# Keys and three gated attention groups turned by VectorE in 32x32 blocks instead of by TensorE

## What is computed

```
q, k, v, gate = split(h @ w_in)                    # 2048, 256, 256, 2048 columns
q, k = rms_norm(q, q_gain), rms_norm(k, k_gain)    # 32 query heads, 4 key heads of 64
s = q . k * 64**-0.5 + bias[dist]                  # window of 128 positions, blocks of 128
m = max(max(s), sink);  p = exp(s - m)
o = (p / (sum(p) + exp(sink - m))) . v
out = x + (o * silu(gate)) @ w_out
```

## Time and profile before

| | |
|---|---|
| median of 3 runs | 1460.72 us |
| profiled execution | 1460.59 us, of it span 1458.9 us |
| TensorE busy, clock | 99% of the span, granted clock 1.0 of full |
| VectorE busy | 66% |
| ScalarE busy | 48% |
| GpSimd busy | 9% |

### The profile page before, as it was taken

The page is one execution under the profiler, slowest core; times in us unless marked ns, Lnnn a source line. Parts: engine busy times, 40 slices in busy tenths (PEclk is TensorE's granted clock), DMA queues, the critical chain, the costliest instruction groups (busy, mean ns, idle before and its releaser), DMA issues.

```text
span 1458.9 us, 18259 instructions
## 1 busy us (share of the span) xinstructions
PE 1447.7 (99%) x6683; PEld 1195.6 (82%) x6683; DVE 964.6 (66%) x1287; ACT 696.7 (48%) x928; POOL 126.6 (9%) x115
## 2 busy tenths in 40 slices
PE   9999999999999999999999999999999999999999
PEld 7887888888888888888888888887878888888887
DVE  5499978856666554566754556769698566665553
ACT  7444564454444443444443444445555566564432
POOL 2099110000000000000000000000000211200000
PEclk9999999999999999999999999999999999999999
DMA  9755655566665566666655666645555655545562
GB/s 332 221 177 156 196 176 203 199 203 188 201 191 198 187 190 195 192 193 195 191 188 195 189 197 191 194 166 180 195 189 187 220 152 175 156 121 165 172 205 93
DMA packets 141495, 274.04 MB, mean 188 GB/s; under 512 B 8593, under 2 KB 10893, under 8 KB 141304
## 3 DMA queue, kind: packets, MB, share of 16 engines
q1 hardware_dynamic: 139608, 266.49, 58.2%
q0 software_dynamic: 1792, 6.71, 1.5%
q10 hardware_dynamic: 32, 0.01, 0.0%
HBM read 271.02 MB, written 2.15 MB: 187 GB/s over the span
## 4 chain that ended last, share of the span: by engine, by line
PE 89%; DVE 9%; ACT 1%; issue 1%; POOL 0%; ACTq 0%; POOLq 0%
PE acc L1240 28%; PE acc L1242 28%; PE acc L1241 28%; DVE w_lo L781 3%; DVE tile L847 2%; DVE tile L805 1%; PE tp L1491 1%; PE acc L1302 1%; PE tp L1260 1%; PE sp L1472 1%; PE tp L1270 1%; DVE tile L1119 0%; DVE yl L816 0%; ACT w_hi L493 0%; ACT tile L702 0%
## 5 line engine op out<-in xcount | busy, mean ns | idle before, releaser
L781 DVE TENSOR_TENSOR w_lo<-w_raw,w_hi 128x1024 fp32r<-128x1024 f32 x500 | 610.8, 1228 | 423.2 <-ACT w_hi L493 421.1
L493 ACT ACTIVATE w_hi<-w_raw 128x1024 fp32r<-128x1024 f32 x500 | 526.4, 1059 | 581.0 <-PE acc L1242 578.4
L1240 PE MATMUL acc<-w_lo,yh 128*128 128x512 f32 x1184 | 462.7, 391 | 3.6 <-DVE w_lo L781 3.6
L1242 PE MATMUL acc<-w_hi,yl 128*128 128x512 f32 x1184 | 460.8, 389 | 0.0
L1241 PE MATMUL acc<-w_hi,yh 128*128 128x512 f32 x1184 | 460.7, 389 | 0.0
L1240 PE MATMUL acc<-w_lo,hh 128*128 128x512 f32 x784 | 310.4, 396 | 0.6 <-DVE w_lo L781 0.6
L1242 PE MATMUL acc<-w_hi,hl 128*128 128x512 f32 x784 | 305.7, 390 | 0.0
L1241 PE MATMUL acc<-w_hi,hh 128*128 128x512 f32 x784 | 305.2, 389 | 0.0
L1240 PEld LDWEIGHTS acc<-w_lo,yh 128*128 128x128 f32 x1184 | 222.2, 188 | 53.0 <-DVE w_lo L781 6.4
L1242 PEld LDWEIGHTS acc<-w_hi,yl 128*128 128x128 f32 x1184 | 222.2, 188 | 46.6
L1241 PEld LDWEIGHTS acc<-w_hi,yh 128*128 128x128 f32 x1184 | 222.3, 188 | 45.7
(11 more groups left out here) (158 smaller groups left out, 612.2 us busy)
## 6 DMA issues: line engine op xcount, KB each, us to landing
w_raw<-in_w_gate SPq DMA_DIRECT2D x88, 512.0 KB, 3.8
w_raw<-in_w_up SPq DMA_DIRECT2D x88, 512.0 KB, 3.9
w_raw<-in_w_down SPq DMA_DIRECT2D x88, 512.0 KB, 3.8
w_raw<-in_swa_w_in SPq DMA_DIRECT2D x72, 512.0 KB, 3.8
w_raw<-in_w_in SPq DMA_DIRECT2D x64, 512.0 KB, 4.3
w_raw<-in_w_out SPq DMA_DIRECT2D x32, 512.0 KB, 3.8
w_raw<-in_w_ple_gate SPq DMA_DIRECT2D x32, 512.0 KB, 4.3
w_raw<-in_swa_w_out SPq DMA_DIRECT2D x32, 512.0 KB, 4.3
```

The lines of the kernel that those rows point to most:

```text
L493: act.activation(w_hi[:, s % SPL], w_raw[:, s % RAW], ACT.Copy).then_inc(hi_ready, 1)
L781: dve.tensor_tensor(w_lo[:, s % SPL], w_raw[:, s % RAW], w_hi[:, s % SPL].bitcast(F32), ALU.subtract).then_inc(lo_ready, 1)
L1240: pe.matmul(dst, xh[:, f, tk], w_lo[:, s % SPL, k], start=(f == 0), stop=False)
L1242: last = pe.matmul(dst, xl[:, f, tk], w_hi[:, s % SPL, k], start=False, stop=(f == CK * n - 1))
```

## The change

The keys are turned by VectorE: after the chunks (2,2) to (2,5) it turns one quarter each of `tok(2)` into tile 3; TensorE's transposes at (2,3) and ScalarE's copies at (2,6) are gone. TensorE waits for `k_turned` before the first scores. The gated groups 0 to 2 are turned by VectorE too: after the chunks c = 4 to 7 of units 6, 7 and 8 it turns one quarter each of group v-6 into tile 5. ScalarE's high part and VectorE's low part come from that tile at c = 1 of the next unit (before: from PSUM at c = 0). TensorE's transposes at (6,5), (7,5) and (8,5) are gone; TensorE waits for the low parts at chunks 0, 2 and 4 of the first output unit. Group 3 is as before. On VectorE, the turn of a chunk stands in front of `softmax_max(3,2)` at (6,5) and of `weighted(3,0)` at (6,6), and `turned_low` at (7,1) in front of `weighted(3,1)`.

```diff
+T_FFN, T_HID, T_PLE, T_SWA, T_OG = 0, 3, 11, 14, 17
...
@@ ScalarE
-                    if (v, c) == (2, 6):
-                        copy(H_K, tile[3])
...
-                    if c == 0 and v >= 7:
-                        high(H_OG[v - 7], yh[:, 4 * (v - 7):4 * (v - 7) + 4])
+                    if c == 1 and v >= 7:
+                        turned_high(T_OG + v - 7, yh[:, 4 * (v - 7):4 * (v - 7) + 4], turned_in=5)
...
-                    if (j, c) == (0, 0):
-                        high(H_OG[2], yh[:, 8:12])
+                    if (j, c) == (0, 1):
+                        turned_high(T_OG + 2, yh[:, 8:12], turned_in=5)
@@ VectorE
-                        last.then_inc(kd_ready, 1)
-                    if c == 0 and v >= 7:
+                        step(last)
+                    if v == 2 and 2 <= c <= 5:
+                        turn(tok(2), (c - 2,), k_turned if c == 5 else None, turn_in=3)
+                    if c == 1 and v >= 7:
                         q = slice(4 * (v - 7), 4 * (v - 7) + 4)
-                        low(H_OG[v - 7], yl[:, q], yh[:, q])
+                        turned_low(T_OG + v - 7, yl[:, q], yh[:, q], turned_in=5)
...
+                    if c >= 4 and v >= 6:
+                        if c == 4:
+                            dve.wait_ge(og_ready, v - 5)
+                        turn(wide[:, :, CW * (v - 6):CW * (v - 5)], (c - 4,), turned if c == 7 else None, turn_in=5)
                     if c == 5 and 3 <= v <= 6:
                         softmax_max(v - 3, 2)
@@ TensorE
+                if n == 0:
+                    pe.wait_ge(k_turned, 1)
...
-                    if (v, c) == (2, 3):
-                        pe.wait_ge(kd_ready, 1)
-                        to_features(H_K, tok(2))
...
-                    if c == 5 and v >= 6:
-                        pe.wait_ge(og_ready, v - 5)
-                        g = v - 6
-                        to_features(H_OG[g], wide[:, :, CW * g:CW * (g + 1)])
...
-                    if (j, c) == (0, 0):
-                        wait_half_left(pe, H_OG[1] + 1)
-                    if (j, c) == (0, 4):
-                        wait_half_left(pe, H_OG[2] + 1)
+                    if j == 0 and c in (0, 2, 4):
+                        pe.wait_ge(turned_lo, T_OG + c // 2 + 1)
```

More of the change, by code:

```diff
@@ L80 @@
 HALVES += "xx"
-H_K = len(HALVES)
-HALVES += "aa"
-H_Q, H_PT, H_PV, H_OG = {}, {}, {}, {}
+H_Q, H_PT, H_PV = {}, {}, {}
 for _g in range(5):
@@ L95 @@
         H_Q[_g] = len(HALVES); HALVES += "aa"
-    else:
-        H_OG[0] = len(HALVES); HALVES += "xx"
     H_PV[q, 1] = len(HALVES); HALVES += "d"
@@ L100 @@
     H_PV[q, 2] = len(HALVES); HALVES += "d"
-for _g in range(1, 4):
-    H_OG[_g] = len(HALVES); HALVES += "xx"
-T_FFN, T_HID, T_PLE, T_SWA = 0, 3, 11, 14
+H_OG = len(HALVES)
+HALVES += "xx"
+T_FFN, T_HID, T_PLE, T_SWA, T_OG = 0, 3, 11, 14, 17
 ROUNDS = ((0, 0, 8, 1), (1, 0, 4, 2), (1, 4, 4, 2))
@@ L263, in build @@
         kv_ready = sem("kv_ready")
-        kd_ready = sem("kd_ready")
         q_squares = sem("q_squares")
@@ L275, in build @@
         turned_lo = sem("turned_lo")
+        k_turned = sem("k_turned")
         stored = sem("stored")
@@ L513, in high, with turned_high @@
                     last.then_inc(feat_hi, 1)
-            def turned_high(n, dst, gains=None, lap=ONCE):
+            def turned_high(n, dst, gains=None, lap=ONCE, turned_in=TURN):
                 act.wait_ge(turned, n + 1 + lap.turns)
                 if gains is None:
-                    last = act.activation(dst, feat(TURN), ACT.Copy)
+                    last = act.activation(dst, feat(turned_in), ACT.Copy)
                 else:
@@ L764, in _ @@
                     if (j, c) == (0, 5):
-                        high(H_OG[3], yh[:, 12:16])
+                        high(H_OG, yh[:, 12:16])
         @block.vector
@@ L796, in low, with turn @@
                     last.then_inc(tp_left["d"], 1)
-            def turn(src, quarters, done=False):
+            def turn(src, quarters, done=None, turn_in=TURN):
                 for q in quarters:
@@ L802, in turn, with turned_low @@
                         block = src[P // 4 * q:P // 4 * (q + 1)].rearrange("p t (k r n) -> p t k r n", k=4, r=4)[:, :, :, r]
-                        into = feat(TURN)[P // 4 * r:P // 4 * (r + 1)].rearrange(
+                        into = feat(turn_in)[P // 4 * r:P // 4 * (r + 1)].rearrange(
                             "p k (t q n) -> p t k q n", t=T, q=4)[:, :, :, q]
                         last = dve.transpose(into, block)
-                if done:
-                    last.then_inc(turned, 1)
-            def turned_low(n, dst, hi, gains=None, lap=ONCE):
+                if done is not None:
+                    last.then_inc(done, 1)
+            def turned_low(n, dst, hi, gains=None, lap=ONCE, turned_in=TURN):
                 dve.wait_ge(turned_hi, n + 1 + lap.turns)
                 if gains is None:
-                    last = dve.tensor_tensor(dst, feat(TURN), hi.bitcast(F32), ALU.subtract)
+                    last = dve.tensor_tensor(dst, feat(turned_in), hi.bitcast(F32), ALU.subtract)
                 else:
@@ L1002, in _ @@
                             wait_left(dve, OUT_UNIT + j - 1)
-                        turn(resid[:, :, CW * (j - 1):CW * j], (0, 1) if c == 4 else (2, 3), c == 5)
+                        turn(resid[:, :, CW * (j - 1):CW * j], (0, 1) if c == 4 else (2, 3), turned if c == 5 else None)
                     if j and c == 6:
@@ L1030, in pair @@
                             wait_left(dve, u - 1, lap)
-                        turn(tok(1), (c - 5,), c == 8)
+                        turn(tok(1), (c - 5,), turned if c == 8 else None)
                     if kt is not None and c == 9:
@@ L1066, in _ @@
                             wait_left(dve, base + 4 + d - 1)
-                        turn(resid[:, :, CW * (d - 1):CW * d], (0, 1) if c == 3 else (2, 3), c == 4)
+                        turn(resid[:, :, CW * (d - 1):CW * d], (0, 1) if c == 3 else (2, 3), turned if c == 4 else None)
                     if d and c == 5:
@@ L1213, in _ @@
                     split(START[SO_UNIT + j] + c)
-                    if (j, c) == (0, 0):
-                        low(H_OG[2], yl[:, 8:12], yh[:, 8:12])
+                    if (j, c) == (0, 1):
+                        turned_low(T_OG + 2, yl[:, 8:12], yh[:, 8:12], turned_in=5)
                     if (j, c) == (0, 3):
@@ L1218, in _ @@
                     if (j, c) == (0, 5):
-                        low(H_OG[3], yl[:, 12:16], yh[:, 12:16])
+                        low(H_OG, yl[:, 12:16], yh[:, 12:16])
                     if j and c == 3:
@@ L1542, in _ @@
                     u = SO_UNIT + j
-                    if (j, c) == (0, 0):
-                        wait_half_left(pe, H_OG[1] + 1)
-                    if (j, c) == (0, 4):
-                        wait_half_left(pe, H_OG[2] + 1)
+                    if j == 0 and c in (0, 2, 4):
+                        pe.wait_ge(turned_lo, T_OG + c // 2 + 1)
                     if (j, c) == (0, 6):
-                        wait_half_left(pe, H_OG[3] + 1)
+                        wait_half_left(pe, H_OG + 1)
                     chunk(START[u] + c, u, c, yh, yl, by_bank=last_bank if (j, c) == (NG - 1, 7) else None)
@@ L1551, in _ @@
                         pe.wait_ge(og_ready, 4)
-                        to_features(H_OG[3], wide[:, :, 3 * CW:])
+                        to_features(H_OG, wide[:, :, 3 * CW:])
 _INS = ["x", "p", "norm_mix_g", "w_in", "sgu_ln_g", "sgu_ln_b", "sgu_w", "sgu_b", "sc_conv_w", "cf_conv_w",
```

## The result

The changed kernel takes 1463.29 us, the median of 21 runs (1460.86 to 1464.41), against 1461.28 us (1460.50 to 1461.73, 21 runs) of the kernel before: ratio 1.0015, 95% interval 1.0008 to 1.0022. The forecast was 1457.4 us, and the measured time lies 4.1 us above the range: not faster, but a little slower, by less than the 0.2% that was set as the bound. One more execution of the changed kernel, among those run beside the later experiments, took 2441.7 us at a mean granted clock of 0.556; it is counted in no comparison.

What follows compares the result with a forecast made beforehand. TensorE was taken as the bound: 3.6 us of transposes leave it, 0.3 us of new wait comes, so 1460.72 - 3.3 = 1457.4 us. The range was 1456.8 to 1459.2 us.

Steps and rivals of the forecast that it cites:

- What bounds the kernel: TensorE, never starved where the change works; transposes of keys and groups 0 to 2 leaving it save 3.6 us.
- rival B: TensorE isn't the bound: its 18% room absorbs the transposes and chunks wait elsewhere, 1460.7 us; chance 0.08.
- The quarters: Four pieces of each VectorE turn, each between two splits: 1.8 us apiece, 29 us for four turns, all hidden.
- Rival A: Quarters slightly longer, 0.2 us each, or walk off by tenths: turn(3,2) waits 1.1 us, 1458.2 us; chance 0.24.
- rival C: VectorE becomes the bound in units 6 to 8; X beyond 1.8 us per quarter, group 1 waits 4X - 1.3; chance 0.06.
- the walk in group 0: VectorE followed place by place from (6,4): weighted(3,1) done at 1319.05, only new TensorE wait 0.3 us at turn(3,2).
- The wait at `turn(3,2)`: At unit 6's end, TensorE's second half of that block waits for weighted(3,1): 0.3 us, bounds 0 and 0.9.
- Groups 1, 2 and the keys: VectorE's other turns: no TensorE wait; leads 1.3 us in group 1, over 4 in group 2, about 3 for keys.
- the range: 1456.8 (full gain, run-to-run 0.3 us below) to 1459.2 us (rival A with a quarter longer by 0.45 us).
- The rival on the slower side: Rival C: longer quarters make VectorE the bound; 1465 us at X = 1, 1478 us at X = 1.8; chance 0.06.

Runs made afterwards that it cites:

- the spread version: Changed kernel with group 0's quarters at (6,4), (6,6), (6,7), (7,0) behind the attention's own work, turned_low(group 0) behind weighted(3,1): 1457.29 us, ratio 0.9974.

## Why the prediction was wrong, point by point

- **What bounds the kernel** was right. Every block of transposes that left TensorE shortened the run by what the start-to-start times said: 3.6 us predicted, 1458.9 - 1455.2 = 3.7 by the spans of the spread version, 3.5 to 3.6 like with like. The room of 18% that rival B gave TensorE by its weight loads isn't there; the Trainium skill's rule on the busy share (Perfetto Trace Analysis, Identifying the Most-Contended Engine) would have misled here.
- **The quarters** took 1.77 to 1.80 us out of `wide`, as in the earlier trace rows. Rival A's and C's longer quarters did not come.
- **The step that failed is the walk in group 0.** It has the right times: it put the split of (6,7) at 1311.7 behind `weighted(3,0)`; the trace has 1310.7, and with the 0.8 to 0.9 us that the keys take off every time there this is the same. It asked what this delay does to the split, to `exp(3,2)` and to the copies for `weigh(3,1)`, and found slack in each. It did not ask who waits for `weighted(3,0)` itself. The answer was in its own words: "For this the second half of `turn(3,2)` waits" was said of `weighted(3,1)`, and `turn(3,1)` waits for `weighted(3,0)` by the same ring of PSUM halves, with 1.4 us of slack against 5.1 us of delay. That wait stood in the sum at nothing, without a reason. Carried through, the walk would have given 3.7 us of wait, and 3.6 - 3.7: no change.
- **What no step had** is the clock. The wait alone eats the gain; the 2.5 us of half clock from inside the wait on make the kernel slower. The wait alone would have put the time at about 1461 us, above the range too. Nothing in the trace of before showed that price in the attention stage: its waits there are 0.4 us at most.
- **The wait at `turn(3,2)`**, predicted at 0.3 us, did not come even where it could (two quarters later). In the changed kernel itself it had no chance, because TensorE was late by then.
- **Groups 1, 2 and the keys** went as walked: no wait anywhere. The smallest lead behind the keys was 2.4 us, at (2,6), where about 3 was forecast, and in group 2 over 4, as forecast. For group 1, in the changed kernel VectorE's split of (8,0) is the first of the two in the first row and ends at 1345.88 + 1.23 = 1347.11; TensorE wants it at 1348.44, 1.33 us later, where 1.3 was forecast:

```profile
1345.88 2.36 DVE L774 TENSOR_TENSOR w_lo<-w_raw,w_hi 128x1024 fp32r<-128x1024 f32 x2
```
```profile
1348.44 0.39 PE L1239 MATMUL acc<-w_lo,hh 128*128 128x512 f32 x1
```

- **A slip in the range.** Its upper end lets each quarter grow by 0.45 us and counts only the wait at `turn(3,2)`. By rival C's own formula group 1 then waits 4 x 0.45 - 1.3 = 0.5 us too, and the end is 1459.7 us, not 1459.2. The result lies above either.
- **The rival on the slower side** had the wrong mechanism. It let VectorE become the bound by quarters that get longer; the loss came from quarters of exactly the expected length in front of one instruction that TensorE needs. The Trainium skill's rule (VectorE: DVE Perf Modes, Rules for kernel authors) gives such transposes to TensorE; the runs say otherwise for this kernel, where four turns on VectorE, well placed, gain 0.26%.

## What to carry to other kernels

When an engine with time to spare gets new work, follow not only its main stream but every instruction behind the new work, and ask of each who waits for it, PSUM halves that it frees among them; a spare engine has no spare time at the place where it hands something back. Put work without a deadline behind the work with one: the same instructions in another order made the difference between 0.15% slower and 0.26% faster. And price a wait of a few us on TensorE above its length when it is the bound, since what follows may run at half clock, as here behind 3.5 us of standing still, though not behind 1.6.

## What the runs showed of the hardware

- While TensorE stood still for 3.5 us the granted clock went to half, and it stayed there 6.8 us, in both kept traces of the changed kernel; it cost 2.5 us here. One of 32 executions of that kernel kept its clock, by its mean of 1.000. After a wait of 1.6 us in the same place the clock stayed at 1.00, and so it did when 15 useless products filled the 3.5 us.
- TensorE waits 2.0 us for `w_lo` at 127 to 129 us of the span, in all ten kept traces. In five of them the clock is at half for some 3 us from there on, in the other five it stays at 1.00. Two rows of the stretches, of the kernel with one quarter moved and of the kernel before, at the same place:

```profile
130.00:135.00 5.00, 5.00 (x16) 3.93 (x16) 5.00 (x7) 1.05 (x1) 4.83 (x5) 0.66 0.59 173
```
```profile
130.00:135.00 5.00, 4.79 (x22) 3.59 (x21) 5.00 (x7) 1.06 (x1) 4.83 (x5) 1.00 0.63 172
```

  From the last chunk ahead of this wait to the attention stage it is 986.1 to 986.3 us in the five traces without the half clock and 986.9 to 987.1 in the five with it, 0.8 us more. That is most of the 1.2 us by which executions of the kernel before differ. What decides whether the clock falls there is not shown.
- A product of two float32 operands of 128x128 takes 0.22 us from start to start and leaves two records (60 for 30 products in 6.7 us); a transpose of the same size by `transpose` takes 0.11 us (four in 1308.02 - 1307.58 = 0.44 us, in the run with 30 products) and leaves one.
- VectorE's transposes of 32x256 take 436 ns in the mean whatever they read (`resid`, a tile or `wide`). Four of them last 1.78 us while TensorE stands still and 1.77 to 1.80 beside running matmuls, and the plain chunks beside them keep their 2.72 us.
